# Attention scores of a prompt on one core: 64 lanes of queries and keys instead of 128 zero-padded lanes

## Time and profile before

| what | us |
|---|---|
| three timed runs | 9058.5, 9095.69, 9100.66 |
| their median | 9095.69 |
| span of the profiled execution, first to last instruction | 9049.5 |

### The profile page before, as it was taken

How to read it: one execution, slowest core, us unless ns; L and a number is a source line. 1 busy time by engine, 2 the same in 40 slices (tenths; PEclk the granted TensorE clock), 3 DMA queues, 4 the chain that set the end, 5 groups by cost and what they waited for, 6 DMA issues and landing times. The chain is left out here.

```text
span 9049.5 us, 108358 instructions
## 1 busy us (share of the span) xinstructions
PE 7671.2 (85%) x34617; PEld 4779.1 (53%) x34617; DVE 5346.9 (59%) x10521; ACT 3105.5 (34%) x5279; POOL 45.5 (1%) x51
## 2 busy tenths in 40 slices
PE   6999999678799997888888878899986896386899
PEld 3444444345566665666556646666654564334544
DVE  2332322467888778777777777777878787121133
ACT  1222222144455454444444434444443442100011
POOL 0000000000000000000000000000000000000000
PEclk8999999789899998999988889989987997697999
DMA  2111111310000000000000000000000000202133
GB/s 101 52 46 47 47 46 52 92 31 22 20 22 22 20 17 15 15 14 14 14 13 13 14 12 14 11 7 14 13 13 10 7 12 3 59 1 60 57 144 123
DMA packets 245830, 295.18 MB, mean 33 GB/s; under 512 B 58180, under 2 KB 208196, under 8 KB 241732
## 3 DMA queue, kind: packets, MB, share of 16 engines
q1 hardware_dynamic: 217844, 263.53, 9.0%
q0 software_dynamic: 4688, 17.04, 0.5%
q10 hardware_dynamic: 22784, 8.40, 0.4%
HBM read 194.56 MB, written 96.42 MB: 32 GB/s over the span
## 5 line engine op out<-in xcount | busy, mean ns | idle before, releaser
L803 ACT ACTIVATE p_PT<-p_TP 128x512 f32<-128x512 f32 (+1 forms) x1712 | 963.1, 580 | 2542.3 <-PE p_TP L746 2542.3
L467 PE MATMUL t_zp<-t_w,t_xT 128*128 128x512 f32 (+1 forms) x3696 | 1443.1, 551 | 42.5 <-DVE t_w L420 42.5
L916 DVE TENSOR_SCALAR_CACHE_REDUCE p_Y<-p_X,p_col 128x512 bf16<-128x512 f32 (+7 forms) x480 | 1256.1, 2617 | 9.3 <-issue 0.8
L746 PE MATMUL p_TP<-p_ident,p_S 128*128 128x128 f32 x6592 | 1044.5, 292 | 161.4 <-ACT p_S L791 161.0
L700 PE MATMUL p_SC<-p_akT,p_q 128*128 128x512 f32 x1440 | 755.4, 665 | 393.0 <-DVE p_mc L852 392.7
L700 PE MATMUL p_SC<-p_ikT,p_q 128*128 128x512 f32 x2304 | 1031.4, 610 | 54.8 <-DMA p_bv<-out_dsa_v 29.2
L746 PEld LDWEIGHTS p_TP<-p_ident,p_S 128*128 128x128 f32 x6592 | 850.7, 159 | 428.9 <-ACT p_S L791 235.1
L467 PEld LDWEIGHTS t_zp<-t_w,t_xT 128*128 128x128 f32 x3696 | 662.4, 192 | 778.3 <-issue 735.4
L791 ACT ACTIVATE p_S<-p_S,p_negm 128x256 f32<-128x256 f32 (+8 forms) x512 | 854.0, 1668 | 422.5 <-DVE p_mjunk L857 420.2
L728 PE MATMUL p_OP<-p_bv,p_PT 128*128 128x64 f32 x6912 | 921.9, 282 | 70.7 <-ACT p_PT L803 70.7
L728 PEld LDWEIGHTS p_OP<-p_bv,p_PT 128*128 128x128 f32 x6912 | 884.2, 201 | 115.8 <-issue 84.5
(11 more groups left out here) (215 smaller groups left out, 5368.8 us busy)
## 6 DMA issues: line engine op xcount, KB each, us to landing
scr_qkT<-t_qT SPq DMA_DIRECT2D x33, 960.0 KB, 3.7
p_biasA<-in_window SPq DMA_DIRECT2D x16, 1280.0 KB, 6.5
t_x<-in_x_prompt SPq DMA_DIRECT2D x32, 512.0 KB, 3.9
f_o<-scr_o SPq DMA_DIRECT2D x32, 512.0 KB, 4.3
f_gate<-scr_gate SPq DMA_DIRECT2D x32, 512.0 KB, 5.3
f_x<-in_x_prompt SPq DMA_DIRECT2D x32, 512.0 KB, 3.6
out_y_p<-f_y POOLq DMA_DIRECT2D x32, 512.0 KB, 4.2
scr_gate<-t_z SPq DMA_DIRECT2D x66, 192.0 KB, 1.9
```

The costliest lines, as they stand in the source:

```text
L467: mm = pe.matmul(zp[(NZ * p + c) % 2][:, 0:n], xT[:, p, k, :], w[:, k, a:a + n], start=(k == 0), stop=(k == KD - 1))
L746: mm = pe.transpose(TP[n % 2][:, b, :], S[:, a % 2, s0 + b * P:s0 + (b + 1) * P], ident[0:R, 0:R])
L803: act.activation(dst, src, ACT.Copy).then_inc(pT_ready.sem, 1)
L916: link(dve.tensor_scalar(GE[:, 0:L], X[:, 0:L], c(MID), None, ALU.is_ge, ALU.add, accum_out=c(CNT)))
```

## The change

Each query of the prompt is kept once, in the lanes of its half, in 12 slots instead of 24. A score product takes the 64 lanes of its half from the query slot and from the keys. The loads write the half's lanes of consecutive slots. Transposes, value products, the waits, the order of the work and the number of instructions are as before. POOL still zeroes the (now smaller) `q`.

```diff
-                            ("q", [P, 24, P]), ("iw", [P, 8]), ("biasA", [P, 5 * 512]), ("causal", [P, 512])):
+                            ("q", [P, 12, P]), ("iw", [P, 8]), ("biasA", [P, 5 * 512]), ("causal", [P, 512])):
...
+    def lanes(half):
+
+        return slice(HD * half, HD * half + HD)
+
+    def query(kind, slot, half, n):
+        return t["q"][lanes(half), slot, :]
+
     def key(kind, slot, half, n, c0, w):
         if kind == "C":
-            return t["ckT"][:, slot - T_CQ, c0:c0 + w]
-        return t[{"I": "ikT", "A": "akT", "B": "bkT"}[kind]][:, c0:c0 + w]
+            return t["ckT"][lanes(half), slot - T_CQ, c0:c0 + w]
+        return t[{"I": "ikT", "A": "akT", "B": "bkT"}[kind]][lanes(half), c0:c0 + w]
...
                 for half in range(2):
-                    sp.dma_start(t["q"][HD * half:HD * half + HD, 2 * lo + half:2 * hi:2, :],
+                    sp.dma_start(t["q"][lanes(half), lo:hi, :],
                                  qkT[bass.ds((TG * g + j) * P + HD * half, HD), lo * P:hi * P]
                                  .rearrange("p (s c) -> p s c", c=P)).then_inc(sems[sem].sem, 16)
...
-    io = {"open": opened, "query": lambda kind, slot, half, n: t["q"][:, 2 * slot + half, :],
-          "key": key, "value": value, "sync": sync, "ident": None, "q": None,
+    io = {"open": opened, "query": query, "key": key, "value": value, "sync": sync, "ident": None, "q": None,
```

## The result

Three timed runs of the changed kernel took 10291.49, 10362.68 and 10423.68 us, median 10362.68, against 9095.69 before. The ratio is 1.140 [1.132, 1.148]: the kernel is 14% slower, and the prediction's range of 8940 to 9225 does not hold it.

A forecast was written before the change was run, and what follows sets the result against it. The prediction took TensorE to set the pace in the prompt's attention, in index and head parts alike. It summed -153 + 111 + 5 = -37 us, from the median 9095.7 to 9059 us, range 8940 to 9225.

The forecast's parts named there:

- The score pass itself: Score passes in the prompt's attention: over 64 lanes they stay 0.430 us apart, worth 0.
- The clock rival: Prompt's attention: half the rows may not raise TensorE's clock from 1.2 GHz, half the stage cold; 10062 us, chance 0.06.
- The index products: Index part of each query tile: passes of alternating halves overlap, VectorE becomes the limit; -153 us, bounds 0 and -191.
- Strict turns: Rival: passes of the two halves never overlap, index products stay at 0.859 us; 9212 us, chance 0.14.
- The changes of shape: Between 64-lane scores and 128-lane work: 0.145 us per tile switch, +111 us for 768 exposed, +5 us entering index products.
- The rival of a whole drain: At each tile switch TensorE waits out the whole pass, then loads weights: 0.30 us each, 9183 us, chance 0.08.
- Weights of a half: Rival for A and B score passes: weights can't load under a same-half pass, 0.14 us each; 9503 us, chance 0.04.
- The absorbed case: Rival: the costs of switching tile shape vanish in waits elsewhere, such as VectorE's work; 8943 us, chance 0.10.
- Loads and set-up: Query loads and zeroing of the slots: same DMAs and bytes, zeroing half as long but covered by key loads; both 0.

The follow-up runs named there:

- at 66 lanes: Kernel before, with all heads' scores over lanes 0 to 65, so no tile shape changes; upper heads used the wrong query: 10182.49 us, ratio 1.118.
- Heads alone: Changed kernel with only the heads' scores at 64 lanes, index products back on 128 padded lanes and 24 query slots: 10500.45 us, ratio 1.148.
- index alone: Changed kernel with only the index products at 64 lanes, heads' scores back on 128 padded lanes and 24 query slots: 8867.87 us, ratio 0.977.

## Why the prediction was wrong

**The step that failed** is the first of its parts, "The score pass itself ... I leave 0.430 us. ... Worth 0". At the full clock it is right: sixteen warm passes over 64 lanes take 7.13 us, (7.13 - 0.59)/15 = 0.436 us apart, against (7.08 - 0.59)/15 = 0.433. What it left out is that the same passes also set the clock under which everything behind them runs. The clock rival said just that and got a chance of 0.06. The argument against it was taken from a row with half the *columns*, and the sentence itself noted that no row has half the *rows*: an unknown with a price of 1000 us was settled by an analogy. Runs at 66, 96 and 128 lanes put the stage's clock at 0.71, 0.86 and 0.90.

**The size of that rival** was 10062, and 10362.68 came. It took half the chunks at the lower clock. A share of 0.68 of the *time* is 0.68/(0.68 + 2 x 0.32) = 0.52 of the *work* if all of it takes twice as long, and 0.20 was 0.20/(0.20 + 2 x 0.80) = 0.11. With its own formula, (0.52 - 0.11) x 1584 x 2.11 = 1370 us; with the -37 of the forecast that is 1333, near the 1380 by which the stage grew. The price of a chunk holds too: a cold head of eight chunks takes 34.14 - 18.15 = 15.99 us more, 2.00 a chunk. So that rival had the mechanism and the price, and its share was too small.

**The index products** were right in mechanism and undersized: -153 was forecast with -191 as the bound, and they gave 166 us between the profiled spans (9049.5 to 8883.8) and (1 - 0.9766) x 9078 = 212 in timed runs, beyond the bound. A likely reason, which no run tests, is that the sum counted only VectorE's end of the chain. TensorE leaves the run of 64 products after 42.30 us instead of 55.15, 12.85 us earlier, and starts the heads then; at that rate 1152 products are an estimated 231 us. Strict turns fell: 42.30/64 = 0.66 us a product. The Trainium skill, "TensorE: Matmul & The Clock Gate", Part 3, says that matmuls in different row groups run concurrently; the trace agrees with this 0.66, where turns give 0.86.

**The changes of shape** were right: 0.145 us each was forecast, 0.116 to 0.166 was measured, and a warm head's period grew from 17.86 to 18.15 us, 0.29 or two changes, where 18.2 had been forecast. The rival of a whole drain (0.30 each) fell. They weigh more at the lower clock: from the last B score pass to the first transpose the kernel after takes 0.52 us warm and 0.99 cold, at 66 lanes 0.43 and 0.85 (medians of its records), so the bare gap is 0.09 us warm and 0.14 cold. Heads alone at 64 lanes, with changes, cost 14.8%, at 66 lanes, without, 11.8%. The 3.0% between them, 272 us against 111, mixes these dearer changes with a clock that is lower still, 0.69 against 0.71, and the runs do not part the two.

**Weights of a half** load under passes of the same half after all: the passes are 0.436 us apart, where that rival had 0.14 us more, and in the records each load, 0.19 us long, lies under the pass of the same half that starts with it. The Trainium skill, "TensorE: Matmul & The Clock Gate", Part 3, says in one place that loads overlap matmuls in flight only where row groups differ; these records are against that.

**The absorbed case** needed the gain without the costs of the heads; it has no support in the trace after. Loads and set-up were not tested by themselves.

**The sum as measured**: -2.3% (index alone) + 11.8% (66 lanes without changes) + 3.0% (changes on top) = +12.5%, and the change has +14.0%. The remaining 1.5%, some 140 us, is more than the intervals of the ratios together (about 1%) and stays open; the parts act on one clock, so they need not add up, and the kernel after also has 12 query slots where these runs keep 24. Open is too what exactly in a pass counts for the clock between 66 and 96 lanes: only these points were run, and with padded lanes that hold zeros.

## What to carry to other kernels

Before narrowing a product to fewer rows of the array, read the granted clock of its stage: if the engine drops to 0.50 at waits, ask which passes bring it back, and try those at full height even if half of it is zeros. Row halves pay where two independent products can alternate between them, as in the index products here; a run that stays in one half gains nothing, and pays two changes of shape. When a rival costs some 25 times what the forecast gains and no row speaks against it directly, its chance should not be small: it should be the first experiment.

## What the runs showed of the hardware

Three things were not expected. Rows in use decide how soon TensorE's clock comes back: at 0.50, 68 of 68 us busy with 64-lane scores, full-height transposes and value products left it there, 64 index passes of one half in 52 us did too, and the arrival of the other half raised it within 6 passes in 15 runs of 16; with 64-lane scores it stayed low for 62 us a time instead of 12. Once up, one half alone held it at 1.00. Passes of two halves overlap around a meeting even when they are queued in blocks of 16, which brings the run to 0.32 us a pass instead of 0.430. And a change of tile shape has a price of its own, 0.12 to 0.17 us, with no effect on the clock (0.89 with a thousand of them).
